# Opening of a two-layer hybrid decoder trunk: packed weight columns, another order of the first loads, short idle matmuls, and a new order of steps

## The chip, the cores and the metric

The kernel runs on one core of a Trainium2 chip. The metric is the device time of one execution in microseconds. The kernel before takes 665.01 us, the median of three runs (664.68, 665.01 and 666.29). The number looked for is the same median for the changed kernel.

## The reference

Two layers, each on 512 tokens of width 1024, all in float32. A layer normalises `h`, multiplies by one combined weight matrix and feeds four attention branches; their gated outputs are concatenated, multiplied by `w_out`, normalised and added to `h`.

```python
for layer in range(DEPTH):                       # DEPTH = 2
    u = rms_norm(h, norm_pre[layer])
    proj = u @ w_in[layer]                       # 1024 x 4200 columns, split into 19 parts
    y_a = mla_branch(...) * silu(a_g)            # latent attention, 4 heads
    y_b = dilated_branch(...) * silu(b_g)        # three dilated windows, 4 heads
    y_c = sparse_branch(...) * silu(c_g)         # 8-head indexer picks the 128 best keys, 4 heads
    y_d = diff_branch(...) * silu(d_g)           # difference of two softmax maps, 4 heads
    y = jnp.concatenate([y_a, y_b, y_c, y_d], axis=-1) @ w_out[layer]
    h = h + rms_norm(y, norm_post[layer])
```

## The kernel before, in words

**Weights.** The columns of `w_in` are taken in 16 groups (GROUPS, L49 to L66) of up to 264 columns, `w_out` in four more. Each group goes through one of three slots: SyncE loads 1 MB into `w_raw` (L532), ScalarE copies it, rounded, to `w_high` (L769), GpSimd subtracts to get `w_low` (L727). The token matrix is split in the same way into two parts of `uT`. A product is three matmuls for each chunk of 128 rows: high by high, high by low, low by high (`three`, L1341). Most groups have two column blocks; one block over eight chunks is 24 matmuls, cut into a "lead" step (chunks 0 to 3) and a "unit" step (chunks 4 to 7). A load takes its rows straight out of `w_in`, in pieces of one DMA for each part of the group: two for "cv" (256 columns and 8), three for "cq" (192, 32 and 32).

**Opening.** Layer 0 starts by FIRST_START (L99). For each of four blocks of 128 tokens: ScalarE squares the block (L787), VectorE makes the mean (L1012), GpSimd the root (L734), VectorE the normalised block `u` (L1027), TensorE eight transposes (L1338), ScalarE and VectorE the high and low parts of `uT` (L800, L1035). In between, group "cv" is applied: "half" is its chunks 0 to 3, "unit cv" its chunks 4 to 7. The gain row is spread over the partitions by two matmuls first (L1366). The first group is loaded in two halves of four chunks and converted by ScalarE (L814) and VectorE (L1100), the first half at step "hnorm 0", the second at step "u 0".

**Order.** Every engine runs the same SEQUENCE of steps and does its part of each; nothing but semaphores ties them. The order is written out by hand in SCHEDULE (L111), one for both layers. "scores j a b" are score blocks of job j (a head of a branch): TensorE multiplies (L1456, L1463, L1459), VectorE shifts and takes the maximum (L1187), ScalarE exponentiates (L882). "turn j k" transposes probabilities (TensorE L1481, ScalarE copies L895), into one of two banks, so turn t waits for the copy of turn t-2. "pv" multiplies by the values (L1500), "norm" is a VectorE step, "wide" (ScalarE) and "spread" (TensorE L1519, then L1208) spread the reciprocals. "topk n" is n rounds of selection on VectorE alone (L1065, L1066), 48 rounds to a layer. "fill" adds the selection to the bias on GpSimd (L752); the scores of job 8 wait for "fill 8", and that for the last "topk". "aweights" and "asplit" round the weights and latents of branch A, "mix" splits the concatenated output. Score blocks use three banks in turn, lead and unit steps two.

Of the kernel before, what the change touches and what calls it, by code (L numbers as in the profile page):

```python
# [40 lines left out]
for _n, _w in (("cq", 192), ("ckv", 128), ("kr", 32), ("ga", 256), ("bq", 256), ("bk", 256), ("bv", 256),  # L41
# [25 lines left out]
NGI = len(GROUPS)  # L67
NGO = 4
# [43 lines left out]
    lead cq 0, lead cq 1, unit cq 0, unit cq 1, lead qi 0, unit qi 0, lead qi 1, unit qi 1, lead dq 0, unit dq 0, lead dq 1, idx 0, unit dq 1, idx 1, lead dv 0, idx 2, unit dv 0, lead dv 1, unit dv 1, idx 3, lead dv 2, idx 4, lead dv 3, idx 5, idx 6, unit dv 2, idx 7, lead dk 0, unit dv 3, topk 3, unit dk 0, topk 1, lead dk 1, topk 2, unit dk 1, lead gd 0, topk 1, unit gd 0, topk 1, lead gd 1  # L112
    scores 0 0 2, topk 1, scores 0 2 5, unit gd 1, lead gb 0, scores 0 5 7, unit gb 0, scores 0 7 8
    scores 1 0 1, lead gb 1, topk 1, norm 0, unit gb 1, turn 0 0, scores 1 1 4, topk 1, turn 0 1, scores 1 4 7, lead ckv 0, topk 3, scores 1 7 8, unit ckv 0, lead bq 0, turn 0 2, topk 2
    scores 2 0 2, turn 0 3, norm 1, unit bq 0, lead bq 1, turn 1 0, scores 2 2 3, turn 1 1, scores 2 3 8, topk 1, norm 2, unit bq 1, turn 1 2, squares_a, topk 2
    scores 3 0 1, turn 1 3, lead bk 0, topk 1, unit bk 0, lead bk 1, topk 1, unit bk 1, topk 1, pv 0, turn 2 0, turn 2 1, scores 3 1 3, dsum 0, scores 3 3 6, topk 1, lead cqq 0, scores 3 6 8, norm 3, wide 0, turn 2 2, turn 2 3, unit cqq 0
    scores 4 0 3, topk 1, spread 0, turn 3 0, topk 2, turn 3 1, lead cqq 1, scores 4 3 4, topk 3, turn 3 2, lead ck 0, turn 3 3, unit cqq 1, topk 1
    scores 5 0 2, turn 4 0, pv 1, unit ck 0, wide 1, turn 4 1, dsum 1, norm 4, topk 1, scores 5 2 4, topk 1, turn 4 2, lead ck 1, norm 5, topk 1, unit ck 1
    scores 6 0 1, lead bv 0, unit bv 0, topk 1, turn 4 3, turn 5 0, asums, topk 1, turn 5 1, wide 2, topk 1, turn 5 2, spread 1, scores 6 1 4, lead bv 1, unit bv 1, turn 5 3, topk 1
    scores 7 0 1, topk 2, lead bv 2, unit bv 2, topk 2, lead bv 3, topk 3, unit bv 3, topk 1, spread 2, scores 7 1 3, lead gc 0, topk 1, fill 8, topk 2, unit gc 0, scores 7 3 4, lead gc 1, unit gc 1, turn 6 0, norm 6, norm 7, pv 2  # L120
    scores 8 0 2, asplit, turn 6 1, turn 6 2, lead ga 0, turn 6 3, wide 3, turn 7 0, aroot, turn 7 1, wide 8, fill 9, spread 3, aload, scores 8 2 4, unit ga 0, fill 10, wide 9, turn 7 2, turn 7 3, akr
    scores 9 0 1, fill 11, scores 9 1 4, pv 3
    scores 10 0 1, aweights, lead ga 1, turn 8 0, turn 8 1, unit ga 1, mix 6, turn 8 2, spread 8, turn 8 3, turn 9 0, turn 9 1, spread 9, norm 8, scores 10 1 3, norm 9, turn 9 2, wide 4, scores 10 3 4, aq 0
    scores 11 0 1, norm 10, ak 0, mix 7, spread 4, turn 9 3, turn 10 0, scores 11 1 4, pv 4, aq 1, aq 2, turn 10 1, turn 10 2
# [161 lines left out]
def trunk(nc, x, w_in, w_out, norm_pre, norm_post, mla_q_norm, mla_kv_norm, mla_w_uq, mla_w_ukv,  # L286
# [8 lines left out]
    with ExitStack() as ctx:  # L295
# [83 lines left out]
        u = [at(f"u{i}", f"probs{i}", [P, DM], F32) for i in range(2)]  # L379
        waste = at("waste", "probs2", [P, DM], F32)  # L380
# [102 lines left out]
        def wait_w_loaded(eng, g):  # L483

            eng.wait_ge(w_loaded[g % SLOTS], 16 * sum(len(GROUPS[i % NG][1]) if i % NG < NGI else 1
                                                      for i in range(g % SLOTS, g + 1, SLOTS)))
# [35 lines left out]
        def _(sp):  # L522
            def load_group(g):
# [5 lines left out]
                if i < NGI:  # L529
                    c = 0  # L530
                    for first, n in GROUPS[i][1]:
                        sp.dma_start(w_raw[:, g % SLOTS, :, c:c + n],  # L532
                                     w_in[l, :, first:first + n].rearrange("(k p) c -> p k c", p=P)
                                     ).then_inc(w_loaded[g % SLOTS], 16)
                        c += n
# [1099 lines left out]
```

## Time and profile before

| what | value |
|---|---|
| median of three runs | 665.01 us |
| profiled execution | 664.22 us |
| its span, first to last instruction | 662.4 us |
| TensorE (PE) busy | 636.5 us, 96% |
| VectorE (DVE) busy | 392.7 us, 59% |
| ScalarE (ACT) busy | 355.8 us, 54% |
| GpSimd (POOL) busy | 241.4 us, 36% |
| mean granted TensorE clock | 0.993 |
| start of "lead cq 0", the first step of SCHEDULE | 29.75 us |

The profiled execution spends 1.8 us outside its span. In the tables of the timeline a row is: start, length, engine, line, operation, output and inputs, shapes, count, and in brackets the idle time of the engine before it with what ended it. Matmuls overlap, so the rate of a row of matmuls is the distance between their starts and not their length. A row of windows gives the stretch, its length, the busy time of each engine with its number of instructions, then the granted clock, the DMA share and GB/s.

### The profile page before, as it was taken

How to read it: one execution, taken by the hardware profiler on the slowest of the kernel's cores; microseconds unless marked ns; L12 is line 12 of the kernel's file. 1: busy time of each engine (PE TensorE's matmuls, PEld its weight loads, DVE VectorE, ACT ScalarE, POOL GpSimd, SP SyncE). 2: the span in 40 equal slices, each digit the busy share in tenths (PEclk: the TensorE clock that was granted, in tenths of full speed). 3: DMA queues.
4: the chain of work that ended last, by engine and by line, in shares of the span. 5: the costliest groups of instructions: out<-in, count | busy, mean ns of one | idle time of the engine just before them, and what ended most of it. 6: DMA issues, size and time to landing. Idle time of an engine off the chain costs nothing. (4 is left out here: it accounts for less than half of the span.)

```text
span 662.4 us, 10348 instructions
## 1 busy us (share of the span) xinstructions
PE 636.5 (96%) x3700; PEld 521.5 (79%) x3700; DVE 392.7 (59%) x986; ACT 355.8 (54%) x818; POOL 241.4 (36%) x209
## 2 busy tenths in 40 slices
PE   6999999999999999999999999999999999999996
PEld 4977887777778767679998897777777876776996
DVE  4322775986868558640381249679787765764124
ACT  4522734585465586862353454456655648678121
POOL 1443343345043781023416433343424359300330
PEclk9999999998999999999999999999999999999999
DMA  8447967553452403212372587644535222130202
GB/s 261 127 138 227 269 206 230 194 160 89 97 140 72 139 1 116 76 28 101 98 223 64 171 261 228 173 137 118 169 84 128 77 82 79 64 128 1 96 33 96
DMA packets 78589, 85.78 MB, mean 129 GB/s; under 512 B 21013, under 2 KB 62229, under 8 KB 78537
## 3 DMA queue, kind: packets, MB, share of 16 engines
q1 hardware_dynamic: 78537, 85.11, 42.9%
q8 instruction: 30, 0.49, 0.3%
q14 instruction: 22, 0.18, 0.1%
HBM read 70.38 MB, written 13.94 MB: 127 GB/s over the span
## 5 line engine op out<-in xcount | busy, mean ns | idle before, releaser
L727 POOL TENSOR_TENSOR w_low<-w_raw,w_high 128x512 fp32r<-128x512 f32 (+2 forms) x156 | 198.9, 1306 | 346.2 <-ACT w_high L769 346.1
L1343 PE MATMUL bank<-uT,w_high 128*128 128x512 f32 x400 | 160.4, 401 | 1.7 <-DVE cqlow L1145 0.9
L1345 PE MATMUL bank<-uT,w_low 128*128 128x512 f32 x400 | 158.6, 397 | 0.0
L1344 PE MATMUL bank<-uT,w_high 128*128 128x512 f32 x400 | 158.3, 396 | 0.0
L882 ACT ACTIVATE probs<-probs,negmax 128x128 f32<-128x128 f32 (+3 forms) x160 | 88.7, 558 | 53.9 <-DVE negmax L1187 52.9
L769 ACT ACTIVATE w_high<-w_raw 128x1024 fp32r<-128x1024 f32 (+2 forms) x78 | 76.4, 1030 | 27.6 <-DMA w_raw<-in_w_out 24.3
L1343 PEld LDWEIGHTS bank<-uT,w_high 128*128 128x128 f32 x400 | 75.8, 189 | 19.6 <-issue 3.3
L1345 PEld LDWEIGHTS bank<-uT,w_low 128*128 128x128 f32 x400 | 75.4, 189 | 17.8
L1344 PEld LDWEIGHTS bank<-uT,w_high 128*128 128x128 f32 x400 | 75.6, 189 | 16.0
L1343 PE MATMUL bank<-w_high,mix 128*128 128x256 f32 x256 | 72.4, 283 | 0.0
L1344 PE MATMUL bank<-w_low,mix 128*128 128x256 f32 x256 | 71.8, 280 | 0.0
L1345 PE MATMUL bank<-w_high,mix 128*128 128x256 f32 x256 | 71.8, 280 | 0.0
L895 ACT ACTIVATE turned<-bank 128x512 f32<-128x512 f32 (+3 forms) x128 | 51.0, 432 | 18.7 <-PE bank L1481 9.3
L1343 PE MATMUL bank<-w_high,uT 128*128 128x256 f32 (+1 forms) x192 | 56.4, 294 | 1.1 <-DVE uT L1035 1.1
L1481 PE MATMUL bank<-ident,probs 128*128 128x128 f32 x320 | 51.8, 277 | 3.9 <-ACT turned L895 2.9
L1345 PE MATMUL bank<-w_high,uT 128*128 128x256 f32 (+1 forms) x192 | 55.2, 288 | 0.0
L1344 PE MATMUL bank<-w_low,uT 128*128 128x256 f32 (+1 forms) x192 | 55.2, 288 | 0.0
L1065 DVE MAX8 best<-select 128x8 f32<-128x512 f32 (+2 forms) x96 | 53.5, 558 | 1.8
L1187 DVE CUSTOM_DVE_ANT_0 probs<-bank,strips 128x128 f32<-128x128 f32 (+1 forms) x104 | 45.5, 472 | 12.2 <-PE bank L1456 8.3
L1066 DVE MATCH_REPLACE8 select<-best,select 128x512 f32<-128x512 f32 (+2 forms) x96 | 52.1, 543 | 0.0
L1481 PEld LDWEIGHTS bank<-ident,probs 128*128 128x128 f32 x320 | 37.8, 140 | 16.6 <-ACT turned L895 8.4
L1343 PEld LDWEIGHTS bank<-w_high,mix 128*128 128x128 f32 x256 | 48.1, 188 | 0.3 <-issue 0.3
(167 smaller groups left out, 1016.8 us busy)
## 6 DMA issues: line engine op xcount, KB each, us to landing
w_raw<-in_w_in SPq DMA_DIRECT2D x27, 1024.0 KB, 5.4
w_raw<-in_w_out SPq DMA_DIRECT2D x8, 1024.0 KB, 4.8
parts_dram<-staging SPq DMA_DIRECT2D x12, 512.0 KB, 6.9
strips<-strips_dram SPq DMA_DIRECT2D x24, 256.0 KB, 4.9
dqk<-parts_dram SPq DMA_DIRECT2D x24, 256.0 KB, 4.2
hX<-in_x SPq DMA_DIRECT2D x8, 512.0 KB, 5.8
qidx<-parts_dram SPq DMA_DIRECT2D x12, 256.0 KB, 4.2
w_raw<-in_w_in SPq DMA_DIRECT2D x4, 512.0 KB, 5.7
```

The lines of the kernel that those rows point to most:

```text
L727: ins = nc.gpsimd.tensor_tensor(w_low[:, s, ks, 0:w], w_raw[:, s, ks, 0:w], w_high[:, s, ks, 0:w].bitcast(F32), ALU.subtract)
L769: nc.scalar.activation(w_high[:, g % SLOTS, ks, 0:w], w_raw[:, g % SLOTS, ks, 0:w], ACT.Copy).then_inc(w_high_done, 1)
L882: nc.scalar.activation(pr, pr, ACT.Exp, bias=negmax[:, j % 4, m, q:q + 1], scale=-1.0, accum_out=sums[:, j % 4, m, q:q + 1]).then_inc(exp_ ...
L895: nc.scalar.activation(turned[j % 2][:, TOFF[kb]:TOFF[kb] + w], bank[:, TURN + t % 2, 0:w], ACT.Copy).then_inc(turn_emptied, 1)
L1065: after(nc.vector.max(best[:], row))
L1066: after(nc.vector.match_replace(row, best[:], row, MARK))
L1187: nc.vector.tensor_tensor_reduce(sl, bank[:, SCORE + n % 3, 0:WID[q]], bias, -1.0, 3.0e38, ALU.add, ALU.min, negmax[:, j % 4, m, q:q + 1]) ...
L1343: nc.tensor.matmul(out_ap, lh, rh, start=start, stop=False)
L1344: nc.tensor.matmul(out_ap, lh, rl, start=False, stop=False)
L1345: return nc.tensor.matmul(out_ap, ll, rh, start=False, stop=stop)
L1481: ins = nc.tensor.transpose(bank[:, TURN + t % 2, (q - kb) * P:(q - kb + 1) * P], buf[:, POFF[q] + kb * P:POFF[q] + (kb + 1) * P], ident[:])
```

## The change

1. `w_in` is laid out ahead of the launch (`packed`), so that the columns of a group stand together, for each partition all eight chunks one behind another. A group is one DMA, whatever its parts.
2. The first loads go in the order: gain row, token block 0, first half of group "cv", identity, token block 1, second half of "cv", token blocks 2 and 3. Before, both halves stood ahead of token block 1.
3. VectorE splits the second half of the weights at step "hnorm 1", behind the normalising of block 1, not at "u 0".
4. GpSimd zeroes a tile `idle`, and TensorE runs three 128x128 float32 matmuls on it at each of three places: ahead of the gain row's matmuls, behind them, and behind the transposes of token block 0. They write to the PV bank, which nothing uses yet.
5. SCHEDULE is written anew for both layers. FIRST_START stays.

```diff
+FIRST_COL = [sum(n for g in GROUPS[:i] for _, n in g[1]) for i in range(NGI)]
...
-    lead cq 0, lead cq 1, unit cq 0, unit cq 1, lead qi 0, unit qi 0, lead qi 1, unit qi 1, lead dq 0, unit dq 0, lead dq 1, idx 0, unit dq 1, idx 1, lead dv 0, idx 2, unit dv 0, lead dv 1, unit dv 1, idx 3, lead dv 2, idx 4, lead dv 3, idx 5, idx 6, unit dv 2, idx 7, lead dk 0, unit dv 3, topk 3, unit dk 0, topk 1, lead dk 1, topk 2, unit dk 1, lead gd 0, topk 1, unit gd 0, topk 1, lead gd 1
-    scores 0 0 2, topk 1, scores 0 2 5, unit gd 1, lead gb 0, scores 0 5 7, unit gb 0, scores 0 7 8
-    scores 1 0 1, lead gb 1, topk 1, norm 0, unit gb 1, turn 0 0, ...
+    lead cq 0, lead cq 1, unit cq 0, unit cq 1, lead qi 0, unit qi 0, lead qi 1, lead dq 0, unit qi 1, unit dq 0, lead dq 1, idx 0, unit dq 1, lead dv 0, idx 1, unit dv 0, lead dv 1, idx 2, unit dv 1, idx 3, lead dv 2, idx 4, idx 5, lead dv 3, idx 6, unit dv 2, idx 7, unit dv 3, topk 2, lead dk 0, topk 2, unit dk 0, topk 1, lead dk 1, unit dk 1, topk 2, lead gd 0, unit gd 0, topk 1, lead gd 1
+    scores 0 0 2, topk 1, scores 0 2 5, topk 1, lead gb 0, scores 0 5 7, topk 1, unit gd 1, unit gb 0, scores 0 7 8
+    scores 1 0 1, topk 1, lead gb 1, norm 0, unit gb 1, turn 0 0, ...
...
-    scores 7 0 1, topk 2, ..., spread 2, scores 7 1 3, lead gc 0, topk 1, fill 8, topk 2, unit gc 0, scores 7 3 4, lead gc 1, unit gc 1, turn 6 0, norm 6, norm 7, pv 2
-    scores 8 0 2, asplit, ...
+    scores 7 0 1, lead bv 3, topk 2, asplit, ..., scores 7 1 3, fill 8, spread 2, topk 2, lead gc 0, turn 5 3, topk 3, unit gc 0, lead gc 1, scores 7 3 4, unit gc 1, turn 6 0
+    scores 8 0 2, pv 2, norm 7, ...
...
-    scores 10 0 1, aweights, lead ga 1, turn 8 0, turn 8 1, unit ga 1, mix 6, turn 8 2, spread 8, turn 8 3, turn 9 0, ...
+    scores 10 0 1, pv 3, lead ga 1, turn 8 0, aweights, turn 8 1, unit ga 1, turn 8 2, mix 6, spread 8, turn 8 3, turn 9 0, ...
...
-    ..., scores 13 2 4, ak 1, turn 11 2, turn 11 3, mix 3, spread 5, mix 2, pv 5, ...
+    ..., ak 1, spread 5, turn 11 2, turn 11 3, scores 13 2 4, mix 3, mix 2, pv 5, ...
...
+        idle = at("idle", "probs3", [P, P], F32)
...
             for tb in range(NB):
                 sp.dma_start(hX[:, tb, :], x[0, tb * P:(tb + 1) * P, :]).then_inc(h_loaded[tb], 16)
+                if tb < 2:
+                    ks = slice(4 * tb, 4 * tb + 4)
+                    sp.dma_start(w_raw[:, 0, ks, 0:WIDTH[0]], group_rows(0, 0)[:, ks, :]
+                                 ).then_inc(w_loaded[0] if tb else half_loaded, 16)
                 if tb == 0:
                     sp.dma_start(ident[:], ident_in).then_inc(ident_loaded, 16)
-                    for half, done in enumerate((half_loaded, w_loaded[0])):
...
+            nc.gpsimd.memset(idle[:], 0.0).then_inc(pool_ready, 1)
...
-                if (l, step) in ((0, ("hnorm", 0)), (0, ("u", 0))):
-                    half = int(kind == "u")
+                if (l, step) in ((0, ("hnorm", 0)), (0, ("hnorm", 1))):
+                    half = step[1]
...
+            def keep_running(n):
+
+                for _ in range(n):
+                    nc.tensor.matmul(bank[:, PV, 0:P], idle[:], idle[:], start=True, stop=True)
+
+            pe.wait_ge(pool_ready, 3)
+            keep_running(3)
             pe.wait_ge(grow_loaded, 16)
...
             ins.then_inc(gspread_ready, 1)
+            keep_running(3)
...
+                if (l, step) == (0, ("u", 0)):
+                    keep_running(3)
...
+def packed(w_in):
+
+    w = w_in.reshape(DEPTH, KC, P, IN_COLS).transpose(0, 2, 1, 3)
+    blocks = [np.concatenate([w[..., a:a + n] for a, n in g[1]], axis=3).reshape(DEPTH, P, -1) for g in GROUPS]
+    return np.concatenate(blocks, axis=2)
```

## Rows read from the trace of the kernel before

**Rows 1.** Page, busy time of each engine, share of the span, instructions.
```profile
PE 636.5 (96%) x3700; PEld 521.5 (79%) x3700; DVE 392.7 (59%) x986; ACT 355.8 (54%) x818; POOL 241.4 (36%) x209
```

**Rows 2.** Timeline of TensorE, opening: start, length, line, tiles, count, idle before.
```profile
2.25 3.75 PE L1366 MATMUL bank<-grow,ones_row 1*128 1x512 f32 x4 [2.25 <-DMA grow<-in_norm_pre]
8.19 1.94 PE L1338 MATMUL bank<-ident,u 128*128 128x128 f32 x8 [2.19 <-DVE u L1027]
11.19 0.56 PE L1343 MATMUL bank<-w_high,uT 128*128 128x264 f32 x1 [1.06 <-DVE uT L1035]
...
15.09 1.97 PE L1338 MATMUL bank<-ident,u 128*128 128x128 f32 x8 [0.92 <-DVE u L1027]
16.71 0.57 PE L1343 MATMUL bank<-w_high,uT 128*128 128x264 f32 x1
...
18.84 0.29 PE L1343 MATMUL bank<-w_high,uT 128*128 128x264 f32 x1
...
29.75 0.40 PE L1343 MATMUL bank<-uT,w_high 128*128 128x512 f32 x1
```

**Rows 3.** Timeline of ScalarE in the opening.
```profile
4.60 1.06 ACT L787 ACTIVATE waste<-hX 128x1024 f32<-128x1024 f32 x1 [2.59 <-DMA hX<-in_x]
...
8.06 1.08 ACT L814 ACTIVATE w_high<-w_raw 128x1056 fp32r<-128x1056 f32 x1 [2.31 <-DMA w_raw<-in_w_in]
...
10.66 1.08 ACT L814 ACTIVATE w_high<-w_raw 128x1056 fp32r<-128x1056 f32 x1
11.63 1.05 ACT L787 ACTIVATE waste<-hX 128x1024 f32<-128x1024 f32 x1
```

**Rows 4.** Timeline of VectorE in the opening.
```profile
6.76 1.28 DVE L1027 SCALAR_TENSOR_TENSOR u<-hX,roots,bank 128x1024 f32<-128x1024 f32 x1 [0.75 <-POOL roots L734]
...
11.77 1.26 DVE L1100 TENSOR_TENSOR w_low<-w_raw,w_high 128x1056 fp32r<-128x1056 f32 x1
12.94 0.15 DVE L1012 TENSOR_SCALAR means<-sumsq 128x1 f32<-128x1 f32 x1
13.76 1.28 DVE L1027 SCALAR_TENSOR_TENSOR u<-hX,roots,bank 128x1024 f32<-128x1024 f32 x1 [0.67 <-POOL roots L734]
...
16.87 0.69 DVE L1035 TENSOR_TENSOR uT<-bank,uT 128x512 fp32r<-128x512 f32 x1 [1.77 <-ACT uT L800]
```

**Rows 5.** Timeline of GpSimd: the split of the second weight group.
```profile
23.47 5.03 POOL L727 TENSOR_TENSOR w_low<-w_raw,w_high 128x512 fp32r<-128x512 f32 x4 [1.76 <-ACT w_high L769]
```

**Rows 6.** Windows: stretch, length, busy of five engines, clock, DMA share, GB/s.
```profile
76.80:80.20 3.40, 2.34 (x13) 1.48 (x12) 3.40 (x6) 2.31 (x5) 0.53 (x1) 1.00 1.01 222
80.30:83.70 3.40, 3.40 (x14) 3.06 (x13) 2.97 (x7) 2.17 (x6) 0.00 (x0) 0.50 1.00 343
402.00:405.40 3.40, 3.37 (x19) 2.77 (x19) 3.40 (x8) 2.15 (x6) 0.00 (x0) 1.00 0.15 51
162.20:165.60 3.40, 3.40 (x10) 2.62 (x9) 1.03 (x3) 1.11 (x6) 2.04 (x2) 0.50 0.00 0
```

**Rows 7.** Timeline of TensorE, layer 0: waits ahead of "turn 9 0" and "pv 5".
```profile
251.35 0.98 PE L1481 MATMUL bank<-ident,probs 128*128 128x128 f32 x7 [0.77 <-ACT turned L895]
272.65 2.37 PE L1500 MATMUL bank<-turned,values 128*64 128x512 f32 x16 [0.62 <-ACT turned L895]
```

**Rows 8.** Timeline of ScalarE ahead of the first of these waits.
```profile
250.41 0.62 ACT L983 ACTIVATE mix<-gate 128x512 fp32r<-128x512 f32 x1
250.93 0.54 ACT L895 ACTIVATE turned<-bank 128x256 f32<-128x256 f32 x2
```

**Rows 9.** VectorE groups by shape, 84 to 200 us: one selection round.
```profile
L1065 DVE MAX8 best<-select 128x8 f32<-128x512 f32 x16 | 11.1, 691 | 0.3
L1066 DVE MATCH_REPLACE8 select<-best,select 128x512 f32<-128x512 f32 x16 | 10.8, 676 | 0.0
```

**Rows 10.** Timeline of GpSimd, "fill 8", and of VectorE, the shift that needs it.
```profile
220.76 2.97 POOL L752 TENSOR_TENSOR probs<-strips,select 128x256 f32<-128x256 f32 x3 [1.19 <-DVE select L1169]
229.22 0.42 DVE L1187 CUSTOM_DVE_ANT_0 probs<-bank,probs 128x256 f32<-128x256 f32 x1
```

More of the change, by code:

```diff
@@ L117 @@
[L117 to L124, printed above, removed]
@@ new lines @@
+    scores 4 0 3, topk 1, turn 3 0, spread 0, turn 3 1, topk 1, scores 4 3 4, topk 1, lead cqq 1, turn 3 2, topk 2, turn 3 3
+    scores 5 0 2, topk 1, lead ck 0, topk 1, norm 4, unit cqq 1, topk 1, turn 4 0, pv 1, unit ck 0, dsum 1, topk 1, turn 4 1, scores 5 2 4, wide 1, turn 4 2, topk 1, wide 2, topk 1, turn 4 3, lead ck 1, norm 5, unit ck 1, lead bv 0, unit bv 0, turn 5 0, topk 1, asums
+    scores 6 0 1, turn 5 1, topk 1, turn 5 2, spread 1, lead bv 1, unit bv 1, topk 1, scores 6 1 4, lead bv 2, topk 1, norm 6
@@ new lines @@
+    scores 7 0 1, lead bv 3, topk 2, asplit, unit bv 2, topk 3, unit bv 3, scores 7 1 3, fill 8, spread 2, topk 2, lead gc 0, turn 5 3, topk 3, unit gc 0, lead gc 1, scores 7 3 4, unit gc 1, turn 6 0
+    scores 8 0 2, pv 2, norm 7, wide 3, turn 6 1, lead ga 0, turn 6 2, turn 6 3, aroot, turn 7 0, wide 8, turn 7 1, fill 9, fill 10, scores 8 2 4, spread 3, norm 8, unit ga 0, wide 9, turn 7 2, aload, turn 7 3
+    scores 9 0 1, fill 11, akr, scores 9 1 4
+    scores 10 0 1, pv 3, lead ga 1, turn 8 0, aweights, turn 8 1, unit ga 1, turn 8 2, mix 6, spread 8, turn 8 3, turn 9 0, turn 9 1, spread 9, scores 10 1 3, norm 9, turn 9 2, wide 4, aq 0, scores 10 3 4
@@ new lines @@
+    scores 11 0 1, norm 10, ak 0, spread 4, turn 9 3, scores 11 1 4, pv 4, turn 10 0, aq 1, mix 7, aq 2, turn 10 1
+    scores 12 0 4, turn 10 2, wide 5, turn 10 3, norm 11
+    scores 13 0 2, norm 12, aq 3, turn 11 0, turn 11 1, ak 1, spread 5, turn 11 2, turn 11 3, scores 13 2 4, mix 3, mix 2, pv 5, turn 12 0, turn 12 1, av 0, norm 13, turn 12 2, turn 12 3
+    scores 14 0 2, turn 13 0, mix 4, wide 6, turn 13 1, av 1, scores 14 2 4, turn 13 2, spread 6
+    scores 15 0 1, turn 13 3, scores 15 1 4, turn 14 0, pv 6, turn 14 1, turn 14 2, turn 14 3, norm 14, mix 5, wide 7, norm 15, ya 0, turn 15 0, mix 0, turn 15 1, ya 2, spread 7, turn 15 2, turn 15 3, ya 1, pv 7, mix 1
@@ L483, in wait_w_loaded @@
         def wait_w_loaded(eng, g):
-            eng.wait_ge(w_loaded[g % SLOTS], 16 * sum(len(GROUPS[i % NG][1]) if i % NG < NGI else 1
-                                                      for i in range(g % SLOTS, g + 1, SLOTS)))
+            eng.wait_ge(w_loaded[g % SLOTS], 16 * (g // SLOTS + 1))
         def wait_w_used(eng, g):
@@ L529, in load_group @@
                 if i < NGI:
[L530 to L535, printed above, removed]
+                    sp.dma_start(w_raw[:, g % SLOTS, :, 0:WIDTH[i]], group_rows(l, i)).then_inc(w_loaded[g % SLOTS], 16)
                 else:
```

25 lines of the change are left out of this document (9 added, 16 removed).

## The prediction, made before the changed kernel was run

> **What bounds the kernel now.** I read the page's busy times first: TensorE is busy 636.5 of 662.4 us, no other engine over 60% [rows 1]. So the time is TensorE's work plus the stretches in which it waits or runs at the lower clock, and everything else counts only through these. Next I read its timeline over the opening [rows 2]. The reader is to see three gaps there (2.19, 1.06 and 0.92 us) and, between them, matmuls that start 0.22 us apart; from 18.84 us they start 0.12 to 0.13 us apart. That is the clock going from 1.2 to 2.4 GHz, after TensorE has worked without a gap since 15.09 us. From 20.66 us on there is no gap until "lead cq 0" at 29.75. Then the windows [rows 6]: the clock is at half in two more stretches of layer 0, each behind a wait of TensorE, for 3.4 us of work. That costs 1.7 us each time. Last, the timelines around the longest waits inside a layer [rows 7, 8]. The waits of the middle are short, under 1.1 us each, and stand in both layers.
>
> The sum below is made against the profiled execution, 664.22 us (span 662.4 and 1.8 around it); the median of the runs is 0.79 above it. I take the difference to be the same afterwards.
>
> **Part 1, loads.** The first weight half reaches ScalarE at 8.06 us, after 2.31 us idle [rows 3]. In the new order it is the second large load; at the pace of the first token block, which is there at 4.60 us [rows 3] after its data have moved for some 2 us, it lands between 6.1 and 6.6; I take 6.2. ScalarE then copies it in 6.2 to 7.3, and VectorE splits it from 8.04, when `u` of block 0 is done (6.76 + 1.28) [rows 4], to 9.3. What is late next is the high part of `uT`, so "half 0" could start at about 10.75, not 11.19. This gain of 0.44 us is worth nothing on the path: "half 0" takes 2.8 us at the low clock and block 1 is only ready at 15.04 (13.76 + 1.28) [rows 2, 4]. Token block 1 lands earlier too, but its square starts at 11.63 right behind the copy of the second weight half (10.66 and 1.08 more), which itself stands behind `uT` of block 0 [rows 3], and this order is not changed. So the load that was moved forward was not the one waited for: 0. One DMA instead of two or three for "cv" and "cq" frees SyncE's queue; no wait of TensorE in the opening is for group 1 or 2, as it has none after 20.66: 0. If that cover were gone, it would be GpSimd's split of group 1 that is late (23.47 + 5.03 = 28.5 [rows 5] against 29.75): 1.25 us of room. It hangs on ScalarE's copy behind `uT` of block 2 and moves forward with the opening, so it keeps most of its room.
>
> **Part 2, the moved split.** The split of 1.26 us at 11.77 no longer stands ahead of the mean of block 1 [rows 4]. ScalarE's square ends near 12.75 (11.63 + 1.05 and the read of the sum), so the mean starts at 12.8, not 12.94: block 1 is ready 0.14 us earlier, at 14.9. The split now follows it and ends at 16.15. Queued behind it on VectorE are the mean of block 2 (1.2 us later than before, still well ahead of its use) and the low part of `uT` of block 1, which waits for ScalarE until 16.87 anyway [rows 4]. Waiting for the split is "unit cv 0", at 16.71 before: free at the low clock; at the full clock the eight transposes end near 15.95 and the split is 0.2 us late.
>
> **Part 3, the idle matmuls.** Not in the trace. Nearest row: four passes over 512 columns in 3.75 us [rows 2], that is 0.21 us for a pass over 128, two passes to a float32 matmul, so 0.43 each, 1.28 us for three at the low clock, 0.64 at the full one. The first three start when the tile is zeroed, about 1.3, and end at 2.6; the gain row is there at 2.25. So the spread gain ends at 6.35 instead of 6.0. `u` of block 0 starts at 6.76 for its root: 0.4 us of room, cost 0 (up to 0.5 if the first of them is slow to start). The next three end at 7.65, before the transposes at 8.19: 0. The last three run 10.1 to 11.4 and hold up "half 0" by 0.2 against before; it then ends near 14.1, before 14.9: 0.
>
> What they may bring is the clock. TensorE would now work unbroken from 8.19 to 14.1 at least; before, 3.75 us unbroken was followed by the rise [rows 2]. So I expect the rise near 12. The question is whether it lasts over the wait for block 1, which at the full clock is longer, from about 13.0 to 14.9. The rows speak both ways: the wait of 1.0 us between two "idx" steps was followed by the low clock in layer 0 (80.3) and not in layer 1 (402.0), and a third, shorter wait was followed by it at 162.2 [rows 6]. The new gap is longer than any of these. Bounds: if the clock stays, the work from 15.09 to 18.84 (3.75 us) takes half, 1.88 less, plus 0.14 of part 2, less 0.2 for the split: -1.8. If it falls again or never rises: -0.14. If the low stretch begins earlier than 15.4 it also ends earlier, which gives back a part. I take -0.8, nearer to the small end, as the rows with a fall are two to one.
>
> The Trainium skill (TensorE: Matmul & The Clock Gate, What's actually happening) has the clock fall back after a stretch in which the engine is idle. By this rule a short gap with dense work on both sides would not bring it down, and the opening would give -1.8. The fall at 80.3, where TensorE had worked for 2.34 of the 3.40 us before [rows 6], disagrees with it; what it would give is the first rival.
>
> **Part 4, the new order.** It moves no work off TensorE; it can only fill waits. One layer has these over 0.6 us, with what the new text puts there:
> "pv 5" waits for the copy of "turn 11 3" (0.62, with the ramp of the first matmul 0.86) [rows 7]. "scores 13 2 4", 1.5 us of TensorE, now stands between. The wait goes; late next is ScalarE with the exponentials. I take -0.6 (0 to -0.86).
> "turn 9 0" waits 0.77 for the copy of "turn 8 2", queued behind the gate's tanh and "mix 6" [rows 7, 8]. "mix 6" now comes behind it, but "turn 9 1" needs the copy after that, which is then 0.5 later. I take -0.2 (0 to -0.8).
> The wait of 1.0 us between two neighbouring "idx" steps stays, as two of them still stand side by side (4 and 5, before 5 and 6): 0 (-0.5 to +0.5), and with it the risk of the fall at 80.3.
> All other moves by a place or two: 0, from -0.5 to +1.4, one selection round of 0.69 + 0.68 us [rows 9].
> Sum -0.8 a layer, -1.6 for two. The tail of the kernel is not touched.
>
> **Sum.** 664.22 - 0.8 (the opening) - 1.6 (the order) = 661.8, and against the median 665.01 - 2.4 = 662.6 us. What a measurement here tells from no change is 0.3%, 2.0 us: 663.0 and 667.0 are the marks.
>
> **Rivals.**
> (a) The clock rises and stays: -1.8 in the opening, and the order gives -0.8 a layer: 665.01 - 3.4 = 661.6; with both waits of rows 7 gone, -1.6 a layer, 660.0. For it: six unbroken microseconds of work, and the stretch of layer 1 that kept its clock. Against it: two falls after shorter gaps. About 660.8 in the middle.
> (b) The order gives nothing, as the waits filled return at the next use of ScalarE or VectorE, which stand in the same steps, and the clock in the opening falls back: 665.01 - 0.14 to - 0.8: 664.5. For it: work is only shuffled, and each bank pair returns the wait one step later, as at "turn 9 1".
> (c) Slower, by VectorE's queue. The new text has three selection rounds among the score blocks of job 0, before there was one, so two rounds, 2 x 1.37 = 2.7 us [rows 9], more stand ahead of the shifts that free the three score banks and of "norm 0". If TensorE waits for these two in each layer, 665.01 + 5.5 - 0.8 = 669.7; if half is hidden, 666.9. It decides once VectorE's idle time between the score blocks of job 0 is used up. Against it: VectorE is idle for 41% of the span [rows 1], and the total of 48 rounds is the same.
> The same on the other queue: "scores 8 0 2" now stands ahead of "pv 2" and comes 2.3 us earlier, and its shift needs "fill 8". That ended at 223.73 and was used at 229.22 [rows 10], 5.5 us of room, so 3.2 remain ("pv 2" is one such step of 16 matmuls as in rows 7, 2.3 us) if the last round isn't late. I count this in (c).
> (d) The idle matmuls delay the gain: beyond 0.4 us each tenth is a tenth, at most 1.3 - 0.4 = 0.9 us: 665.01 + 0.9 - 1.6 = 664.3 with the order's gain. It lies inside (b) in time.
>
> **How the numbers follow.** The forecast 0.38 (its own range 661.4 to 663.8), (a) 0.20, (b) with (d) 0.29, (c) 0.13. Of the forecast about four fifths lie under 663.0, (a) all: 0.30 + 0.20 = 0.50 faster. Within 0.3%: the rest of the forecast 0.08, (b) 0.28, and 0.03 of (c): 0.39. Slower 0.11. The range takes in (a) with both waits gone at the lower end, 659.2, and (c) half hidden at the upper one, 666.6.
>
> **What would show it.** Right: TensorE's timeline with the rise of the clock near 12 us, a gap before the transposes of block 1, these at about 14.9, and "lead cq 0" between 28.0 and 29.5; "pv 5" with no idle time ahead of it in both layers; the wait between "idx" 4 and 5 still 1 us. Wrong: block 1 transposed before 14.5 (then the loads were on the path after all); `u` of block 0 after 6.8 (the idle matmuls cost); "lead cq 0" at 29.6 or later (the clock gave nothing); waits over 1 us for "norm" or shifts in job 0 and 1, or VectorE waiting for "fill 8". The clock's falls in the middle come and go between executions, 1.7 us each, and could hide an effect as large as the opening's.

## The result, and the profile after

The changed kernel takes **667.92 us** (median of 22 runs, 664.74 to 670.69), the one before on the same chip 664.75 us (22 runs, 661.61 to 666.73). The ratio is **1.0053, 95% interval 1.0038 to 1.0068**: slower by 3.2 us between the medians and 3.5 by the ratio, where 2.4 us less were forecast. The profiled execution of after took 666.04 us, its span is 664.3 us.

A number that profiles of single executions hide does much of the work below. Each run lists its mean granted clock; (1 - clock) x span, called the clock loss here, says how much an execution spends at half clock. Its mean over the runs is 3.9 to 4.4 us for the kernel before (five sets of 17 to 35 runs; the 22 runs beside the changed kernel list no clock) and **6.15 us for the one after**, some 2 us more. Within the 24 sets of runs that list a clock (365 executions), an execution with 1 us more of clock loss took 0.8 us longer (least squares within the sets, error 0.04), so this is about half of the 3.5 us. The opening is not in it: the clock column of the windows stands at 1.00 from the first microsecond of every trace, also where the matmuls of [rows 2] start 0.22 us apart, and the record of the clock begins only with the first rise. In the opening the clock is therefore read from the distance between matmuls.

The page after, busy times: TensorE is busy 1.2 us longer than before [rows 1] (18 passes of idle matmuls are among it) in a span that is 1.9 us longer.

```profile
PE 637.7 (96%) x3718; PEld 523.6 (79%) x3718; DVE 390.8 (59%) x986; ACT 357.2 (54%) x818; POOL 239.6 (36%) x210
```

TensorE's timeline, opening (against [rows 2]):

```profile
1.25 1.65 PE L1365 MATMUL bank<-idle 128*128 128x128 f32 x6 [1.25 <-POOL idle L713]
2.82 3.78 PE L1371 MATMUL bank<-grow,ones_row 1*128 1x512 f32 x4
...
9.88 1.42 PE L1365 MATMUL bank<-idle 128*128 128x128 f32 x6
11.03 0.40 PE L1342 MATMUL bank<-w_high,uT 128*128 128x264 f32 x1
11.26 0.28 PE L1343 MATMUL bank<-w_low,uT 128*128 128x264 f32 x1
11.38 0.28 PE L1344 MATMUL bank<-w_high,uT 128*128 128x264 f32 x1
...
14.93 1.10 PE L1337 MATMUL bank<-ident,u 128*128 128x128 f32 x8 [2.18 <-DVE u L1026]
16.10 0.39 PE L1342 MATMUL bank<-w_high,uT 128*128 128x264 f32 x1
```

From 11.26 the matmuls start 0.12 us apart and not 0.22: the clock is up between 11.03 and 11.26, and it stays up over the gap of 2.18 us, as the eight transposes behind it take 1.10 us. "lead cq 0" starts at 28.21, 1.54 us earlier than [rows 2]. So the opening looks like rival (a). ScalarE and VectorE there (against [rows 3, 4]):

```profile
6.32 1.08 ACT L813 ACTIVATE w_high<-w_raw 128x1056 fp32r<-128x1056 f32 x1 [0.89 <-DMA w_raw<-in_w_in]
11.60 1.05 ACT L786 ACTIVATE waste<-hX 128x1024 f32<-128x1024 f32 x1
```

```profile
12.77 0.15 DVE L1011 TENSOR_SCALAR means<-sumsq 128x1 f32<-128x1 f32 x1 [1.32 <-ACT waste L786]
14.79 1.25 DVE L1099 TENSOR_TENSOR w_low<-w_raw,w_high 128x1056 fp32r<-128x1056 f32 x1
```

Then the lead goes. It is 1.60 us at "idx 0" (60.93 against 62.53), and at the last matmul of "idx 7" the changed kernel is 1.39 us **behind**; in layer 1 the same stretch takes it from 0.13 us behind to 2.81 behind. Here the one wait of before (first fence, row of the kernel before) has become two (second fence, after), in both layers:

```profile
78.35 1.36 PE L1432 MATMUL bank<-kidx,qidx 96*128 96x512 f32 x3 [1.01 <-ACT probs L873]
```

```profile
74.50 0.38 PE L1440 MATMUL bank<-kidx,qidx 96*128 96x256 f32 x1 [0.88 <-ACT probs L872]
76.12 1.56 PE L1440 MATMUL bank<-kidx,qidx 96*128 96x512 f32 x3 [1.24 <-ACT probs L872]
...
399.74 1.56 PE L1440 MATMUL bank<-kidx,qidx 96*128 96x512 f32 x3 [1.24 <-ACT probs L872]
```

Windows of the kernel after (columns as in [rows 6]) show what follows: half clock for 6.83 us in layer 0, and for 3.41 us in layer 1, where there was none at this place before [rows 6].

```profile
72.54:75.95 3.41, 1.47 (x9) 0.89 (x7) 3.41 (x3) 1.32 (x3) 2.56 (x2) 1.00 0.91 271
75.95:82.78 6.83, 6.66 (x27) 6.16 (x28) 5.64 (x12) 3.73 (x9) 0.00 (x0) 0.50 1.04 284
396.81:400.22 3.41, 1.29 (x5) 0.42 (x3) 3.41 (x5) 1.45 (x3) 1.90 (x2) 1.00 1.03 218
400.22:403.63 3.41, 3.36 (x15) 3.20 (x15) 3.41 (x7) 1.88 (x5) 0.00 (x0) 0.50 1.07 314
```

Ahead of both falls VectorE (third pair) is busy for the whole 3.41 us: it adds up the "idx" scores, three sums to a step, and ScalarE may not overwrite the four tiles that it adds from. Its sums by shape, at 70.7 to 75.2 us and again from 76.8 us:

```profile
L1158 DVE SCALAR_TENSOR_TENSOR select<-probs,wi,select 128x512 f32<-128x512 f32 x1 | 1.7, 1714 | 1.9 <-ACT probs L872 1.9
L1158 DVE SCALAR_TENSOR_TENSOR select<-probs,wi,select 128x384 f32<-128x384 f32 x1 | 1.6, 1637 | 0.0
L1158 DVE SCALAR_TENSOR_TENSOR select<-probs,wi,select 128x256 f32<-128x256 f32 x1 | 1.5, 1482 | 0.0
...
L1158 DVE SCALAR_TENSOR_TENSOR select<-probs,wi,select 128x512 f32<-128x512 f32 x2 | 1.5, 740 | 0.0
L1158 DVE SCALAR_TENSOR_TENSOR select<-probs,wi,select 128x256 f32<-128x256 f32 x3 | 1.4, 473 | 0.0
L1158 DVE SCALAR_TENSOR_TENSOR select<-probs,wi,select 128x384 f32<-128x384 f32 x2 | 1.2, 607 | 0.0
```

The same sum takes 1.0 us more in the first stretch. That is where GpSimd splits a weight group (69.31 to 75.1):

```profile
69.31 5.79 POOL L726 TENSOR_TENSOR w_low<-w_raw,w_high 128x512 fp32r<-128x512 f32 x4 [7.79 <-ACT w_high L768]
```

Before, two sums a layer fall into this split (1646 and 1502 ns), after three. The third alone is not the difference: with the spaced first lines of e8 and e12 below, three sums are slow as well (1707, 1643 and 1489 ns in e12), and TensorE waits 0.91 us once a layer. Only with "idx" 4 and 5 side by side right behind does the second wait, of 1.24 us, follow. The Trainium skill (SBUF — State Buffer, Who interferes with whom) says that VectorE and GpSimd share a pair of ports as a lock held for a whole instruction, and that a VectorE instruction with two inputs in SBUF takes part when GpSimd's reads SBUF too. By this rule such sums wait for one piece of the split each; the trace agrees (+1.0 us whatever the width). No run took the split away, so this stays a reading.

Last, "pv 5", without the wait of [rows 7] as predicted; and a new wait near "turn 9 0", in which "spread 8" now waits for the gate:

```profile
271.44 1.67 PE L1467 MATMUL bank<-aqk 128*128 128x384 f32 x4
273.04 2.16 PE L1508 MATMUL bank<-turned,values 128*64 128x512 f32 x12
```

```profile
252.98 0.63 PE L1527 MATMUL bank<-ident,wide 128*128 128x128 f32 x4 [0.72 <-DVE gate L1125]
```

### The profile page after: what moved, and what is told of

It is laid out like the page before. It is cut to its first block and busy times, and to the rows that moved or that the text cites. A ratio compares the mean times of both kernels' runs of the same rounds, so it can differ in the third digit from the quotient of the medians.

```text
span 664.3 us, 10377 instructions
## 1 busy us (share of the span) xinstructions
PE 637.7 (96%) x3718; PEld 523.6 (79%) x3718; DVE 390.8 (59%) x986; ACT 357.2 (54%) x818; POOL 239.6 (36%) x210
## 5 line engine op out<-in xcount | busy, mean ns | idle before, releaser
L1342 PEld LDWEIGHTS bank<-uT,w_high 128*128 128x128 f32 x400 | 75.1, 188 | 19.7 <-issue 2.4
L1343 PEld LDWEIGHTS bank<-uT,w_high 128*128 128x128 f32 x400 | 75.2, 188 | 16.0
```

Of the source, the lines that this page charges most:

```text
L1342: nc.tensor.matmul(out_ap, lh, rh, start=start, stop=False)
L1343: nc.tensor.matmul(out_ap, lh, rl, start=False, stop=False)
```

## The experiments

Each kernel ran 12 times (e14, e15, e18: 6), beside 17 to 35 runs of the kernel before on the same chip. "Clock loss" is the mean of (1 - clock) x span, against that of before in the same batch.

In the column "first line", "new" is the changed kernel's and "spaced" is one made for the experiments; the other lines of SCHEDULE are sixteen (the expectations say fifteen).

| run | opening | first line | other lines | ratio (95%) | clock loss, before |
|---|---|---|---|---|---|
| after | idle, loads, packed | new | new | 1.0053 (1.0038-1.0068) | 6.15 |
| e1 | idle, loads, packed | old | old | 1.0033 (1.0015-1.0051) | 4.99, 4.08 |
| e2 | old | new | new | 0.9991 (0.9971-1.0011) | 5.04, 4.08 |
| e3 | idle, loads, packed | old | new | 0.9991 (0.9974-1.0008) | 3.82, 4.08 |
| e4 | old | new | old | 1.0016 (0.9999-1.0034) | 5.10, 4.08 |
| e5 | e1, one store on ScalarE's queue | old | old | 1.0051 (1.0029-1.0073) | 5.40, 4.42 |
| e6 | idle only | old | old | 1.0007 (0.9982-1.0032) | 4.60, 4.42 |
| e7 | packed only | old | old | 1.0029 (1.0006-1.0051) | 5.66, 4.42 |
| e8 | idle, loads, packed | spaced | new | 1.0005 (0.9988-1.0023) | 4.43, 4.42 |
| e9 | idle, loads | new | new | 1.0028 (1.0007-1.0049) | 5.60, 3.89 |
| e10 | old | old | new | 0.9983 (0.9964-1.0003) | 3.81, 3.89 |
| e11 | idle, loads | old | new | 0.9998 (0.9973-1.0022) | 4.37, 3.89 |
| e12 | old | spaced | new | **0.9964 (0.9941-0.9987)** | 2.10, 3.89 |
| e13 | idle only | spaced | new | 0.9981 (0.9961-1.0001) | 2.87, 4.39 |
| e14 | old, strips store cut | spaced | new | 1.0109 (1.0083-1.0135) | 7.60, 4.39 |
| e15 | idle, strips store cut | spaced | new | 1.0110 (1.0084-1.0135) | 8.39, 4.39 |
| e16 | loads only | old | old | 0.9996 (0.9978-1.0013) | 4.76, 4.39 |
| e17 | old | spaced | old | 1.0014 (0.9989-1.0038) | 3.60, 4.30 |
| e18 | old, rest of store later still | spaced | new | 1.0109 (1.0074-1.0144) | 6.71, 4.30 |

**First batch: opening and order apart, first line apart from the rest.** Edits: e1 is after with the whole old SCHEDULE, e2 before with the whole new one; e3 is after, and e4 before, with the whole first line exchanged. Besides the "idx" part shown here, the lines differ in the place of "unit qi 1" and in the selection rounds behind "idx 7":

```diff
-    ..., idx 0, unit dq 1, lead dv 0, idx 1, unit dv 0, lead dv 1, idx 2, unit dv 1, idx 3, lead dv 2, idx 4, idx 5, lead dv 3, idx 6, unit dv 2, idx 7, ...
+    ..., idx 0, unit dq 1, idx 1, lead dv 0, idx 2, unit dv 0, lead dv 1, unit dv 1, idx 3, lead dv 2, idx 4, lead dv 3, idx 5, idx 6, unit dv 2, idx 7, ...
```

> The changed kernel with the SCHEDULE of before: loads, moved split and idle matmuls alone. Theory A (the loss sits in the first line of the new order, where eight idx steps follow each other too closely for VectorE, and the clock falls behind the wait): the opening's 1.5 us stay, so about 663.2 against 664.75 for before, ratio 0.997 to 0.999; lead cq 0 at 28.2 us. Rival B (the earlier rise of the clock only shifts where it falls later, so the opening pays its gain back): no gain, ratio 1.000 or above.

> The kernel before with the new SCHEDULE alone. Theory A: it loses what the changed kernel lost plus the opening's gain, 3.2 + 1.5 = 4.7 us, ratio 1.006 to 1.008. Rival B: it loses less than the changed kernel, ratio 1.002 to 1.005, as the opening is part of the loss.

> The changed kernel with the first line of SCHEDULE (lead cq 0 to lead gd 1) as before, all other lines new. Theory A: the pair of idx steps waits 1.2 us again and not 2.5, the clock falls less often, nearly all of the loss is gone: 662 to 664, ratio 0.996 to 1.000. Rival C (the loss comes from the other lines, from VectorE's rounds and norms in the middle): still 1.003 or more.

> The kernel before with only the first line of SCHEDULE new. Theory A: two waits of 1.0 and 1.5 us inside the idx steps of both layers in place of one of 1.2, 1.3 us more a layer, and up to 1.7 us more for a fall of the clock in each: 2.6 to 6 us, ratio 1.004 to 1.009. Rival C: ratio under 1.003.

The opening alone makes it slower, as rival B of e1 had it, though it too is 1.57 us ahead at "lead cq 0" (28.18). In its trace the lead is gone at "idx 0", where TensorE waits for the third load of the stacked query parts, as it does before (first row, kernel before), but longer, and starts 0.26 us later:

```profile
62.53 0.77 PE L1432 MATMUL bank<-kidx,qidx 96*128 96x512 f32 x3 [0.64 <-DMA qidx<-parts_dram]
```

```profile
62.79 0.76 PE L1440 MATMUL bank<-kidx,qidx 96*128 96x512 f32 x3 [2.47 <-DMA qidx<-parts_dram]
```

The order alone makes no difference that shows; neither expectation of e2 had that. With the old first line the changed kernel is level with before, as theory A of e3 said: the first line costs it 0.6%, and 0.2% without the new opening (e4, less than the 0.4% that theory A had there; its interval takes in no change).

**Second batch: parts of the opening.** e5 issues the strips store (1.28 MB) from ScalarE's queue and loads the mask later; e6 adds only the idle matmuls to before, e7 only the packed layout; e8 is after with a first line in which no two "idx" adjoin:

```diff
-    ..., idx 1, unit dv 0, lead dv 1, idx 2, unit dv 1, idx 3, lead dv 2, idx 4, idx 5, lead dv 3, idx 6, unit dv 2, idx 7, unit dv 3, topk 2, ...
+    ..., idx 1, lead dv 0, idx 2, unit dv 0, lead dv 1, idx 3, unit dv 1, idx 4, lead dv 2, idx 5, unit dv 2, idx 6, lead dv 3, idx 7, unit dv 3, lead dk 0, topk 3, ...
```

> The opening-only kernel, with the 1.3 MB store of the D strips issued from ScalarE's queue instead of SyncE's and the load of the mask behind that of the first index stack. Theory D (the opening's 1.6 us are lost at idx 0, where the wait for qidx, 2.5 us against 0.6 before, is set by the store of the parts, which stands on the queue behind the strips store): the wait at idx 0 goes to under 0.5 us, idx 0 at 59.5 to 60.5 us instead of 62.8, about 2 us faster than opening only, 664.5 to 665.5, ratio 0.997 to 1.000. Rival F (the strips store takes the same DMA engines whatever the queue): idx 0 at 62 or later, ratio as for opening only, 1.002 to 1.005.

> The kernel before with the nine idle matmuls alone. Theory E (the idle matmuls bring the rise of the clock forward and nothing else in the opening matters): lead cq 0 at 28.2 to 28.8 us, and the time as for opening only, ratio 1.002 to 1.004. Rival G (packed weights or the order of loads are what makes opening only slower): ratio 0.998 to 1.001.

> The kernel before with packed weights alone, one DMA for a group, old order of the first loads, no idle matmuls. Theory E: no change, ratio 0.999 to 1.001, lead cq 0 within 0.3 us of 29.75. Rival G: ratio 1.002 or more.

> The changed kernel with another first line of SCHEDULE, in which no two idx steps stand side by side: idx 0, unit dq 1, idx 1, lead dv 0, idx 2, unit dv 0, lead dv 1, idx 3, unit dv 1, idx 4, lead dv 2, idx 5, unit dv 2, idx 6, lead dv 3, idx 7, unit dv 3. Each idx has at least 1.44 us of matmuls behind it and takes 0.52 itself, against 1.67 us of VectorE for its sums. Theory A: no wait over 0.3 us inside the idx steps, no fall of the clock there: 1.2 us a layer and up to 1.7 for each fall saved against e3, 661 to 664, ratio 0.994 to 0.998. Rival: VectorE stays behind and the wait only moves to the scores of job 0: ratio as e3, 0.999.

SyncE's queue is not the cause (e5 is no faster than e1, at 61.88 "idx 0" still waits 1.54). e6 has "lead cq 0" at 28.16, waits 1.98 us at "idx 0" and gains nothing. The surprise is e7: the layout alone costs 0.3%. Two kinds of DMA (KB of each, median us from issue to landing), first in the kernel before up to 62 us, then in e7 up to 65 us:

```profile
parts_dram<-staging SPq DMA_DIRECT2D x2, 512.0 KB, 7.6
mask<-strips_dram SPq DMA_DIRECT2D x1, 256.0 KB, 4.6
```

```profile
parts_dram<-staging SPq DMA_DIRECT2D x2, 512.0 KB, 8.4
mask<-strips_dram SPq DMA_DIRECT2D x1, 256.0 KB, 5.0
```

The load of the mask takes 4.6 or 4.7 us in thirteen of the fourteen unpacked kernels (4.9 in e17) and 5.0 to 5.2 in after, e1, e3, e7 and e8; the first store of the parts lands after 6.7 to 7.3 us in the unpacked ones and 7.5 to 7.7 in those five. In e7 the third query load lands 26.5 us after the table's store (38.3 to 64.8), before 24.8 (37.6 to 62.4), and TensorE waits for it:

```profile
64.95 1.30 PE L1428 MATMUL bank<-kidx,qidx 96*128 96x512 f32 x3 [2.38 <-DMA qidx<-parts_dram]
```

e8 takes back nearly all of the loss, though it misses the 0.994 to 0.998 expected of it. Its "idx" steps still wait, once a layer for 0.9 us. What it is rid of is the second wait and the fall right behind: its profile falls at 105 and 163. The profiles of all twenty kernels agree. Near 400 us, behind the "idx" waits of layer 1, the clock fell in all four with the new first line (after, e2, e4, e9: 399.1 to 402.5) and in none of the other sixteen. In turn, the four have no fall near 162 or 481, where eight of the nine with the old line have at least one.

**Third batch: packing undone, best use of the order.** e9 is after unpacked, e10 before with the sixteen other lines, e11 is e9 with the old first line, e12 is e10 with the spaced first line.

> The changed kernel with one part undone: the weights lie as before and a group is again loaded in one piece for each of its column ranges. Load order, moved split, idle matmuls and the whole new SCHEDULE stay. Theory G (the packed layout is what makes it slower; by itself it gave 1.0029 in an earlier run, and the idle matmuls by themselves 1.0007, the new order by itself 0.9991): 665.5 us, ratio about 1.000, between 0.998 and 1.002, and distinctly under the changed kernel's 667.9. Rival H (it is the meeting of the earlier opening with the new first line and the idx steps, whatever the layout): 667 us or more, ratio 1.003 to 1.005.

> The kernel before with the new SCHEDULE except its first line, which stays old; opening and layout of before. Theory: the first line with its three close idx steps takes back what the other fifteen lines give, so this is the best use of the new order: 664.0 us, ratio 0.996 to 0.999, with pv 5 and turn 9 0 without their waits and the idx wait 1.0 us once a layer as before. Rival (b) of the prediction (the waits filled return one use later, the order gives nothing anywhere): 665.5, ratio 0.999 to 1.001. VectorE's queue as the cause of slowness: 667 or more, with waits over 1 us in jobs 0 to 2.

> The changed kernel without packing and with the old first line of SCHEDULE: load order, moved split, idle matmuls, and the other fifteen lines new. If both causes (packing and first line) hold and add up: 664.0 us, ratio 0.996 to 0.999. If only the first line counts: as the run with packing and the old first line, 665.3 us, ratio 0.999. If the lead of the opening (about 1.5 us at lead cq 0) could be kept with the old layout, 662.5.

> The kernel before with the new SCHEDULE but a first line of its own, in which every two idx steps have a lead or a unit step between them. If the wait between close idx steps and the fall of the clock behind it are the first line's cost: 663.5 us, ratio 0.995 to 0.998, and no fall of the clock near 78 and 400 us. If the wait of an idx is set by VectorE's three sums (1.67 us for one idx) and spacing only cuts it into two of about 0.9, as in the changed kernel with this line: as with the old first line, ratio 0.998 to 1.000.

The 1.0028 of e9 lies between its two theories. e11, unpacked with the old first line, is no faster than e3, the same with packed weights (0.9998 against 0.9991), where both causes together had promised 0.996 to 0.999. e12 beats both kernels: 662.87 us against 664.99. Its clock loss (2.10 against 3.89) is 1.8 us less, and its mean 1.9 us lower. It has a wait of 0.91 before an "idx" as well, but no fall behind it:

```profile
77.75 0.39 PE L1432 MATMUL bank<-kidx,qidx 96*128 96x256 f32 x1 [0.91 <-ACT probs L873]
79.39 1.34 PE L1432 MATMUL bank<-kidx,qidx 96*128 96x512 f32 x3
```

**Fourth and fifth batch: the chain of transfers, the rest of the opening.** e13 is e12 with the idle matmuls. e14 and e15 are e12 and e13 with the strips store cut; e18 puts the second part behind the second parts' loads and loads the strips at "idx 6". e16 is before with the new order of the loads and the moved split. e17 is before with the spaced line alone. The edits of e14:

```diff
-                    spread_rows(STRIP_ROW["D"], 13)
+                    spread_rows(11, 13)
...
                         sp.dma_start(dst.bitcast(F32), src).then_inc(stack_loaded[s], 16)
+                    if l == 0 and s == 0:
+                        spread_rows(STRIP_ROW["D"], 11)
```

> The kernel of e12 (before, with the new order and a first line whose idx steps are spaced) with the idle matmuls added; layout, loads and split as before. Theory A (the lead is absorbed where idx 0 waits for the third load of the query parts): lead cq 0 near 28.2, idx 0 after a wait of 1.5 to 2.5 us, time as e12 within noise, 662.9 us, ratio 0.995 to 0.998. Rival (the lead carries through): 661.3 us, ratio 0.994. Rival (the wait invites a fall of the clock, so the lead costs): 664.5 us, ratio 0.999.

> The kernel of e12 with one store cut in two: of the five rows of shifted strips that are stored at unit cq 1 (1.28 MB, until about 52 us), only two go then (the mask needs one of them), and the other three behind the first three loads of the query parts, waited for at idx 0. Theory A: the parts store, which stands behind this store on the same transfer engines, lands in 5 to 6 us and not in 7.1, the third query part 1 to 2 us earlier, and the wait at idx 0 (0.6) goes; without the early clock rise that is worth 0.6 us at most, so 662.3 us, ratio 0.994 to 0.998. Rival: a store of two rows runs on two engines as long as one of five does, so the parts store waits for these two as before: no change to e12, parts landing still 7.1 us.

> e14 with the idle matmuls added: lead cq 0 near 28.2. Theory A: with the strips store out of the chain, the lead of 1.5 us gets through idx 0 (start near 60.8 or earlier, wait under 0.7), 661 us, ratio 0.993 to 0.996, and distinctly under e13. Rival: as e13, the wait at idx 0 is still 1.5 us or more, because the chain of store and load has its own time of 25 us from the table's store on.

> The kernel before with only the new order of the first loads and the split at hnorm 1; layout, schedule as before, no idle matmuls. If this part is what costs: 666.5 us or more, ratio 1.002 to 1.004. If it is worth nothing, as the prediction has it (0 for the loads, 0.14 for the split): ratio 0.998 to 1.001, with the transposes of block 1 at about 14.9.

> The kernel before with only its first SCHEDULE line changed: every two idx steps have a lead or a unit step between them (dv leads and units drawn in between). If the spacing is what made e12 faster: 663.3 us, ratio 0.995 to 0.998. If the other fifteen lines gave it (0.9983 with the old first line in e10): ratio 0.999 to 1.001. Both half: 0.9985. The waits between idx steps, 1.0 us once a layer before, go to two of about 0.9 or vanish.

> The kernel of e12, with the strips store cut as in e14, but its last three rows stored behind the loads of the second query parts (about 67 us) and the loads of the strips moved from idx 0 to idx 6. Theory A: the third query part lands near 60 us as in e14, idx 0 starts without a wait on it and idx 4 without e14's 9.8 us; the time is e12's or up to 1 us less, 662.3 us, ratio 0.994 to 0.998. Rival: the three rows, on few transfer engines, hold up the next parts (dq, dk) as they did the second ones in e14, and TensorE waits for those: 666 us or more, ratio 1.001 or more.

e17, at 1.0014, lies beyond both of its expectations: the spaced line alone gains nothing. So e12 owes its time to the other lines or to both together, and its interval overlaps that of e10, which has the old first line; that spacing adds anything to e10 is not shown.

In e13 the idle matmuls bring "lead cq 0" to 28.08 and the run is no faster than e12. e14 shows that the chain of store and loads sets "idx 0": with the lighter store ahead of it the third query load lands at 59.9 and "idx 0" starts at 60.06 with no wait. But the other three rows then hold up the store of the second query parts. ScalarE waits for that store 12.38 us before it may write to `staging` again (first row), the copies of the "idx" scores stand behind it, and "idx 2" waits 9.76 us:

```profile
74.19 0.60 ACT L861 ACTIVATE staging<-bank 128x512 fp32r<-128x512 f32 x1 [12.38 <-DMA parts_dram<-staging]
```

```profile
60.06 0.75 PE L1436 MATMUL bank<-kidx,qidx 96*128 96x512 f32 x3
63.45 0.70 PE L1436 MATMUL bank<-kidx,qidx 96*128 96x512 f32 x3
75.33 1.33 PE L1436 MATMUL bank<-kidx,qidx 96*128 96x512 f32 x3 [9.76 <-ACT probs L877]
```

e18 moves that wait to the weights (4.0 us at 99.22 for a `w_low` of GpSimd). e14 and e15 went as neither of their expectations said: the wait at "idx 0" went, and a longer one came behind it. e18 had the time of its rival. e16 is worth nothing, as the prediction said, but its opening is the lesson: **without idle matmuls** the clock rises at 13.75 and the transposes of block 1 run at full speed (1.09 us and not 1.97 [rows 2]); "lead cq 0" starts at 28.19.

```profile
10.73 0.56 PE L1345 MATMUL bank<-w_high,uT 128*128 128x264 f32 x1 [0.65 <-DVE uT L1037]
14.92 1.09 PE L1340 MATMUL bank<-ident,u 128*128 128x128 f32 x8 [1.21 <-DVE u L1029]
```

Of the ten kernels profiled without idle matmuls, before among them, three had the early rise (13.75 to 14.2: e10, e14, e16; the others 18.8 to 20.2); e10 and e14 have the very opening of before. With them all ten rose at 10.4 to 12.9, and two fell again at 15 (e3, e15). So the lead of 1.5 us is partly luck that the kernel before has too, in about three executions of ten by these profiles.

**Where a lead ends.** Not all at "idx 0". Six unpacked kernels started "lead cq 0" by 28.2 (e6, e9, e10, e11, e13, e16); their "idx 0" starts at 61.24 to 62.28, 61.6 in the mean. Six that started it at 29.75 or later (before, e2, e4, e12, e17, e18) have it at 62.53 to 63.49, mean 63.0. The chain of transfers moves with the lead, from its first store on (35.9 to 36.1 against 37.6 to 38.2), and 1.4 of 1.9 us get through. A second chain takes more in e6. At its first score block (102.77) it is still 1.1 us ahead of before (103.88). At 142.45 it is 2.3 us behind (the same step is at 140.12 before). In between TensorE waits for a split of weights whose 1 MB load, issued at 108.0 beside the 2 MB store of strips, lands 16.9 us later:

```profile
124.96 2.01 ACT L771 ACTIVATE w_high<-w_raw 128x1024 fp32r<-128x1024 f32 x2 [5.41 <-DMA w_raw<-in_w_in]
```

```profile
131.16 0.49 PE L1345 MATMUL bank<-uT,w_high 128*128 128x512 f32 x1 [3.15 <-POOL w_low L729]
```

A wait of about 0.9 us or more for this split stands between 128 and 133 us in eleven of the twenty profiles, the changed kernel's among them (0.94), and in none of before, e10 and e16. No run took this chain away, and each profile is one execution: that it is what eats the lead in the median is not shown.

**Taken together.** Least squares over the fifteen ratios that mix only these parts (all but e5, e14, e15, e18), in per cent with standard errors: new first line **+0.31** (0.06), the other lines **-0.27** (0.06), packed layout **+0.20** (0.07), idle matmuls +0.14 (0.08), load order with the moved split +0.02 (0.07), spaced first line -0.02 (0.07). The sum for the changed kernel is +0.40, measured +0.53. The fit leaves somewhat more scatter than the runs' own errors explain (17 where 9 would be expected), so the parts may not be quite additive; the packed layout and the idle matmuls in particular are small against it. The single comparisons scatter as much: packing is +0.29 in e7 against before and +0.25 in after against e9, but -0.07 in e3 against e11.

## Why the prediction was wrong

**Part 4, the "idx" pair, is the step that failed.** It said: the wait "stays, as two of them still stand side by side ... : 0 (-0.5 to +0.5), and with it the risk of the fall". It looked at which steps adjoin, not at how many sums VectorE still had to make. The new line brings "idx" 3, 4 and 5 closer and a third sum under GpSimd's split; 1.01 us became 0.88 + 1.24 in each layer, and the fall behind them, 3.4 us in one layer before, became 6.83 in one and 3.41 in the other. Measured: +0.31%, 2.1 us, in place of 0. In the profile this is 1.1 us of wait a layer and 3.4 us at half clock more in each; the direct sum, 2 x (1.1 + 1.7) = 5.6 us, is more than the runs bear out. A part of it is that the fall at 162 of before is gone in after, which takes off 1.7 us; the rest stays open. Nor did a run part the "idx" steps of the new line from its moved selection rounds.

**Part 4, the other lines, was right in size, and in part by luck.** -0.6 and -0.2 a layer, -1.6 for two, against -0.27%, 1.8 us. "pv 5" lost its wait. "turn 9 0" shows no wait of 0.77 now, but 0.26 there, 0.72 at the spread behind it and 0.47 behind that: this term gave nothing at its place. And the idle time as a whole did not shrink. From "lead cq 0" of layer 1 to the end, with no fall but in the last 2 us (first row before, second e12, which has the spaced first line too), TensorE's share without work is 12.0 us in both, and the 1.0 us less is in its busy time, where matmuls overlap:

```profile
353.90:662.43 308.53, 296.49 (x1720) 241.88 (x1718) 182.96 (x469) 163.20 (x382) 109.72 (x91) 1.00 0.39 117
```

```profile
355.36:662.88 307.52, 295.52 (x1720) 241.46 (x1718) 181.74 (x469) 163.94 (x382) 108.92 (x91) 1.00 0.40 118
```

Rival (c), VectorE's queue in job 0, did not come: no wait over 1 us for a shift or a norm there.

**Part 3: the early rise came, the gain did not.** -0.8 was forecast as a gain carried to the end. "lead cq 0" came 1.54 us earlier, nearer to the bound of -1.8. But the idle matmuls alone give +0.14% (0.9 us, with an error of 0.5), not -0.12%. Two things failed. A part of the lead isn't theirs, as the rise comes early in some executions anyway. And "from 20.66 us on there is no gap until lead cq 0" was read as if nothing behind "lead cq 0" could absorb a lead, while the 0.64 us that TensorE waited at "idx 0" before already said that a chain of DMAs is the later of the two there. In the led kernels this wait is 0.5 to 2.5 us, and in e6 3.15 us more are waited at 131. Which of these waits counts in the median stays open.

**Part 1: packing isn't free, by most of the comparisons.** "One DMA instead of two or three ... frees SyncE's queue; no wait of TensorE in the opening is for group 1 or 2: 0." The cover named was right for those two groups, and the load order is worth nothing as said (+0.02%). The price is +0.20% (error 0.07), 1.3 us, and the one thing that the traces show longer is other transfers. Why they take 0.4 us longer beside packed weights was not settled; each group is still 1 MB.

**Part 2** was right: mean at 12.77 (12.8 said), split at 14.79, block 1 transposed at 14.93.

**The range** had its upper end at 666.6 from rival (c) half hidden, though the rival's own sum for that, 665.01 + 2.7 - 0.8, is 666.9. No rival joined a loss from the first line with one from the transfers.

## What to carry to other kernels

Before counting a lead at the head of a kernel, go to the places behind it where the bound engine waits for a transfer, or nearly does, and ask at each whether that chain starts earlier by the same amount and runs as fast: what it doesn't give is waited there. Space the steps of a chained accumulation by the time of the engine that drains them, in its slowest neighbourhood, and do not count only which of them adjoin. And compare the mean clock loss over all runs, not the falls in one profile.

## What the runs showed of the hardware

- A VectorE sum with two inputs in SBUF took 1.0 us more (473, 607, 740 ns became 1482, 1637, 1714) while GpSimd split weights.
- TensorE's clock held its full level over a gap of 2.18 us at 12.7 to 14.9 in after, and fell near 15 in e3 over one of 2.23 in the same opening; it fell at 400.2 in after behind a stretch in which TensorE was busy for 1.29 of 3.41 us.
- A store with a small outer dimension held up what followed. In e14 three rows of strips, stored behind the query loads, stretched the store of the next parts from 8.6 us (e13, 56.8 to 65.4) to 12.4 (61.8 to 74.2). A 1 MB load of weights issued behind the 2 MB store of strips took 14.4 us in the kernel before and 16.9 in e6; the load ahead of that store took 6.0 before. The Trainium skill (DMA: Bandwidth & Descriptors, Why a DMA increments its semaphore by 16 and not by 1) says that a DMA is dealt to the largest number of engines, up to 16, that divides the slowest dimension of both sides: five for the first strips store, eight for the second, three in e14. The traces agree: while the first strips store was the only large transfer, the DMA share (second last column) was 0.29 in the kernel before (5 of 16 are 0.31) and 0.14 in e14, where it had two rows (2 of 16 are 0.125):

```profile
41.00:42.50 1.50, 1.50 (x8) 1.21 (x7) 0.00 (x0) 0.01 (x1) 0.00 (x0) 1.00 0.29 105
```

```profile
39.50:40.70 1.20, 1.20 (x6) 0.97 (x6) 0.00 (x0) 0.00 (x0) 0.00 (x0) 1.00 0.14 46
```
